# First weight block and tokens loaded, split and multiplied in four pieces; low parts of the next two blocks made by an adding DMA

## The reference

```python
def _rmsnorm(x, g):
    y = x * lax.rsqrt(jnp.mean(x * x, axis=-1, keepdims=True) + EPS)
    return y * g

def _swiglu(xn, w_in, w_out):
    gu = xn @ w_in                        # 1024 x 5632
    g, u = gu[..., :D_FF], gu[..., D_FF:]
    return (jax.nn.silu(g) * u) @ w_out

def _layer(x, ...):
    x = x + 0.5 * _swiglu(_rmsnorm(x, norm_ffn1), w_ffn1_in, w_ffn1_out)
    ...   # mLSTM, gated linear attention, conv + RG-LRU, merged through w_out
    x = x + 0.5 * _swiglu(_rmsnorm(x, norm_ffn2), w_ffn2_in, w_ffn2_out)
```

## Time and profile before

| | us |
|---|---|
| median of three runs | 3015.81 |
| profiled execution | 3016.17 |
| its span, first to last instruction | 3014.0 |
| PE busy | 2953.7 (98%) |
| DVE busy | 2272.4 (75%) |
| ACT busy | 1340.8 (44%) |
| POOL busy | 12.9 |

### The profile page before, as it was taken

One profiled execution on the slowest core, in us unless ns is written; L12 is line 12 of the kernel. 1 busy time (PEld: TensorE's weight loads), 2 busy tenths in 40 slices (PEclk: granted clock), 3 DMA queues, 4 the chain that ended last, 5 costly groups with the idle time before them and its releaser, 6 DMA issues.

```text
span 3014.0 us, 59955 instructions
## 1 busy us (share of the span) xinstructions
PE 2953.7 (98%) x24960; PEld 2904.6 (96%) x24960; DVE 2272.4 (75%) x3371; ACT 1340.8 (44%) x1733; POOL 12.9 (0%) x36
## 2 busy tenths in 40 slices
PE   8999999999999999999999999999999999999998
PEld 8999999999999999999999999999999999999997
DVE  8685777778788878585785857776878888695766
ACT  5463533334335655363553635333334466453543
POOL 1000000000000000000000000000000000000000
PEclk9999999999999999999999999999999999999999
DMA  3222332323222222232322323233222222222322
GB/s 131 104 98 91 98 109 97 131 96 112 99 89 94 80 83 85 94 103 84 104 78 98 106 97 98 95 127 122 94 93 96 94 91 91 86 78 91 112 84 72
DMA packets 60151, 292.73 MB, mean 97 GB/s; under 512 B 9385, under 2 KB 12265, under 8 KB 32073
## 3 DMA queue, kind: packets, MB, share of 16 engines
q1 hardware_dynamic: 45344, 241.43, 23.7%
q10 hardware_dynamic: 13984, 48.48, 4.4%
q0 software_dynamic: 656, 0.52, 0.1%
HBM read 268.90 MB, written 21.50 MB: 96 GB/s over the span
## 4 chain that ended last, share of the span: by engine, by line
PE 85%; DVE 9%; ACT 3%; issue 1%; DMA 1%; DVEq 0%; ACTq 0%; POOL 0%; POOLq 0%
PE stream_b L477 23%; PE stream_a L477 23%; PE mix L546 11%; PE stream_b L546 6%; PE stream_a L546 5%; PE stream_a L624 5%; PE mix L477 3%; DVE wl L1449 1%; PE mix L909 1%; PE stream_b L630 1%; PE mix L745 1%; PE mix L685 1%; DVE wl L1528 1%; PE mix L829 1%; PE mix L666 1%
## 5 line engine op out<-in xcount | busy, mean ns | idle before, releaser
L1449 DVE TENSOR_TENSOR wl<-stage,wh 128x2048 fp32r<-128x2048 f32 (+1 forms) x148 | 332.7, 2248 | 91.2 <-ACT wh L969 67.0
L969 ACT ACTIVATE wh<-stage 128x2048 fp32r<-128x2048 f32 (+1 forms) x134 | 252.1, 1882 | 318.6 <-PE stream_b L477 221.7
L477 PE MATMUL stream_a<-xh,wh 128*128 128x272 f32 x1280 | 271.0, 293 | 15.6 <-DVE xl L1455 13.2
L477 PE MATMUL stream_b<-xh,wh 128*128 128x272 f32 x1280 | 276.1, 297 | 0.0
L477 PE MATMUL stream_a<-xl,wh 128*128 128x272 f32 x1280 | 265.5, 289 | 0.0
L477 PE MATMUL stream_a<-xh,wl 128*128 128x272 f32 x1280 | 264.9, 288 | 0.0
L477 PE MATMUL stream_b<-xl,wh 128*128 128x272 f32 x1280 | 264.9, 288 | 0.0
L477 PE MATMUL stream_b<-xh,wl 128*128 128x272 f32 x1280 | 264.2, 288 | 0.0
L477 PEld LDWEIGHTS stream_a<-xh,wh 128*128 128x128 f32 x1280 | 202.6, 189 | 18.6 <-DVE wl L1449 13.1
L477 PEld LDWEIGHTS stream_b<-xh,wh 128*128 128x128 f32 x1280 | 201.8, 188 | 7.3 <-issue 3.3
L477 PEld LDWEIGHTS stream_a<-xh,wl 128*128 128x128 f32 x1280 | 201.9, 189 | 0.0
(11 more groups left out here) (435 smaller groups left out, 8598.1 us busy)
## 6 DMA issues: line engine op xcount, KB each, us to landing
stage<-in_w_mix SPq DMA_DIRECT2D x88, 1024.0 KB, 4.9
stage<-in_w_up SPq DMA_DIRECT2D x87, 1024.0 KB, 4.9
stage<-in_w_down SPq DMA_DIRECT2D x16, 1024.0 KB, 5.0
stage<-in_w_down SPq DMA_DIRECT2D x32, 512.0 KB, 4.5
stage<-in_w_down SPq DMA_DIRECT2D x16, 768.0 KB, 4.4
CS<-in_c ACTq DMA_DIRECT2D x8, 1024.0 KB, 4.8
out_o_sc<-CS ACTq DMA_DIRECT2D x8, 1024.0 KB
CS<-in_s ACTq DMA_DIRECT2D x8, 1024.0 KB, 4.9
```

The source lines that it names most:

```text
L477: mm = [pe.matmul(out(h), a(h), b(h), start=f, stop=z) for h in range(2)]
L969: act.activation(wh[:, slot, 0:width], stage[:, slot, 0:width], ACT.Copy).then_inc(hi_done, 1)
L1449: tt_(wl[:, slot, 0:width], stage[:, slot, 0:width], wh[:, slot, 0:width].bitcast(F32), ALU.subtract).then_inc(split_done, 1)
```

## The change

SP now issues the first loads, behind that of the vectors: block 0 in four pieces of two k steps and the tokens in four pieces of two k steps, by turns. ACT no longer issues them; its first instruction is a tiny copy, which brings the first load of its function table forward. ACT and DVE split piece by piece, first two k steps of weights, then two of tokens. TensorE takes block 0 k step by k step, both output tiles in each, when that k step's low token part is there (`first_low`), and sums the squares inside block 1 (`second_block`) and no longer inside block 0.

DVE splits block 1 before it adds the squares from the third on, and ACT makes the high part of block 1 after the third square.

For blocks 2 and 3 of this first network (`f == 0`), ACT writes the negated high part into `wl` and then the high part into `wh`. POOL waits for the first of these and issues a DMA that adds `stage` onto `wl` in SBUF, waits until it has landed, and counts `split_done`. DVE's two subtractions of 128 x 2048 are gone there.

```diff
+FIRST = 4
+FIRST_K = KT // FIRST
...
         def _(sp):
             sp.dma_start(V[:], vec).then_inc(vec_loaded, 16)
+            for p in range(FIRST):
+                piece = slice(p * FIRST_K * 2 * P, (p + 1) * FIRST_K * 2 * P)
+                sp.dma_start(stage[:, 0, piece], w_up1[0, 0][:, piece]).then_inc(
+                    first_loaded[p] if p < FIRST - 1 else block_loaded[0], 16)
+                part = slice(p * FIRST_K, (p + 1) * FIRST_K)
+                sp.dma_start(x[:, part, :], x_T[:, part, :]).then_inc(x_loaded[p], 16)
...
-                        sp.wait_ge(x_loaded[1], 16)
+                        sp.wait_ge(x_loaded[FIRST - 1], 16)
                         load(1, 1, w_up[L, 1])
...
             pool.dma_start(m0t[:], m0).then_inc(const_loaded, 16)
+            for k in range(2):
+                pool.wait_ge(minus_high, k + 1)
+                pool.dma_start(wl[:, k, :], stage[:, k, :], accum_op=ALU.add).then_inc(lows_landed, 16)
+                pool.wait_ge(lows_landed, k * 16 + 16)
+                pool.wait_ge(hi_done, k + 3)
+                pool.memset(token[:, k:k + 1], 0.0).then_inc(split_done, 1)
...
-            def first_block(n, t, j, norm):
+            def first_block(n, t, j):
+                for k in range(KT):
+                    pe.wait_ge(first_low, k + 1)
+                    for e in range(2):
+                        tile(t + e, e, KT, 2 * P, e * P, weights=(wh[:, j], wl[:, j]), ks=[k])
+
+            def second_block(n, t, j, norm, root):
                 parts = (wh[:, j], wl[:, j])
                 block_ready(n)
-                tile(t, 0, KT, 2 * P, 0, weights=parts, low=first_low)
-                tile(t + 1, 1, KT, 2 * P, P, weights=parts, ks=range(KT // 2))
+                tile(t, 0, KT, 2 * P, 0, weights=parts, out=four[2], free=2, ks=range(2))
                 pe.wait_ge(acc_ready, norm)
                 norm_squares().then_inc(norm_sum, 1)
-                tile(t + 1, 1, KT, 2 * P, P, weights=parts, ks=range(KT // 2, KT))
+                tile(t, 0, KT, 2 * P, 0, weights=parts, out=four[2], ks=range(2, KT))
+                pe.wait_ge(sd_ready, root + 1)
+                tile(t + 1, 1, KT, 2 * P, P, weights=parts, out=four[3], free=2)
...
             act.wait_ge(init_done, 1)
-            act.dma_start(stage[:, 0, :], w_up1[0, 0]).then_inc(block_loaded[0], 16)
-            for h in range(2):
-                part = slice(h * (KT // 2), (h + 1) * (KT // 2))
-                act.dma_start(x[:, part, :], x_T[:, part, :]).then_inc(x_loaded[h], 16)
+            act.activation(sdT[:], sdT[:], ACT.Copy)
...
-            def split_hi(nh, slot, through, width):
+            def split_hi(nh, slot, through, width, minus=False):
                 act.wait_ge(block_loaded[slot], nh * 16 + 16)
                 act.wait_ge(tile_done, through + 3)
+                if minus:
+                    act.activation(wl[:, slot, 0:width], stage[:, slot, 0:width], ACT.Copy,
+                                   scale=-1.0).then_inc(minus_high, 1)
                 act.activation(wh[:, slot, 0:width], stage[:, slot, 0:width], ACT.Copy).then_inc(hi_done, 1)
...
+            first_pieces()
+            first_squares(range(3))
+            act.wait_ge(block_loaded[1], 16)
+            act.activation(wh[:, 1, :], stage[:, 1, :], ACT.Copy).then_inc(hi_done, 1)
+            first_squares(range(3, KT))
...
-                                split_hi(nh + 1, i, t + 2 * i + 1, 2 * D)
+                                split_hi(nh + 1, i, t + 2 * i + 1, 2 * D, minus=f == 0)
...
-                        split_lo(n + 2, 0, 2 * D)
+                        if f:
+                            split_lo(n + 2, 0, 2 * D)
...
-                        split_lo(n + 3, 1, 2 * D)
+                        if f:
+                            split_lo(n + 3, 1, 2 * D)
```

More of the change, by code:

```diff
@@ L153, in trunk @@
         zero_t = sb("zero_t", [P, 1])
+        token = sb("token", [P, 2])
         acc = sb("acc", [P, N])
@@ L257, in trunk @@
         const_loaded = sem("const_loaded")
-        x_loaded = [sem("x_loaded_0"), sem("x_loaded_1")]
+        x_loaded = [sem(f"x_loaded_{p}") for p in range(FIRST)]
+        first_loaded = [sem(f"first_block_loaded_{p}") for p in range(FIRST - 1)]
+        first_high = sem("first_high_parts")
+        minus_high, lows_landed = sem("minus_high_parts"), sem("low_parts_landed")
         vec_loaded = sem("vec_loaded")
@@ L511, in norm_squares @@
                 return mm
-            def first_block(n, t, j, norm):
+            def first_block(n, t, j):
[4 more added lines that the diff above has]
+            def second_block(n, t, j, norm, root):
                 parts = (wh[:, j], wl[:, j])
                 block_ready(n)
-                tile(t, 0, KT, 2 * P, 0, weights=parts, low=first_low)
-                tile(t + 1, 1, KT, 2 * P, P, weights=parts, ks=range(KT // 2))
+                tile(t, 0, KT, 2 * P, 0, weights=parts, out=four[2], free=2, ks=range(2))
                 pe.wait_ge(acc_ready, norm)
                 norm_squares().then_inc(norm_sum, 1)
-                tile(t + 1, 1, KT, 2 * P, P, weights=parts, ks=range(KT // 2, KT))
+                tile(t, 0, KT, 2 * P, 0, weights=parts, out=four[2], ks=range(2, KT))
+                pe.wait_ge(sd_ready, root + 1)
+                tile(t + 1, 1, KT, 2 * P, P, weights=parts, out=four[3], free=2)
             def ffn_in_block(L, n, t, j, norm=None, rooted=None):
                 if norm == KT:
-                    return first_block(n, t, j, norm)
+                    return first_block(n, t, j)
+                if rooted == (1, 0):
+                    return second_block(n, t, j, KT, 0)
                 block_ready(n)
@@ L976, in _, with first_pieces @@
             act.wait_ge(vec_loaded, 16)
-            def first_high(slot):
-                act.wait_ge(block_loaded[slot], 16)
-                act.activation(wh[:, slot, :], stage[:, slot, :], ACT.Copy).then_inc(hi_done, 1)
+            def first_pieces():
+                for p in range(FIRST):
+                    piece = slice(p * FIRST_K * 2 * P, (p + 1) * FIRST_K * 2 * P)
+                    act.wait_ge(first_loaded[p] if p < FIRST - 1 else block_loaded[0], 16)
+                    act.activation(wh[:, 0, piece], stage[:, 0, piece], ACT.Copy).then_inc(
+                        first_high if p < FIRST - 1 else hi_done, 1)
+                    act.wait_ge(x_loaded[p], 16)
+                    for m in range(p * FIRST_K, (p + 1) * FIRST_K):
+                        high_part(m, V_FIRST + m)
             def first_squares(ms):
@@ L1727, in _ @@
             dve.wait_ge(vec_loaded, 16)
-            split_lo(0, 0, 2 * D)
-            for m in range(KT // 2):
-                low_part(m, V_FIRST + m, m, first_low)
+            for p in range(FIRST):
+                piece = slice(p * FIRST_K * 2 * P, (p + 1) * FIRST_K * 2 * P)
+                if p < FIRST - 1:
+                    dve.wait_ge(first_high, p + 1)
+                else:
+                    dve.wait_ge(hi_done, 1)
+                ins = tt_(wl[:, 0, piece], stage[:, 0, piece], wh[:, 0, piece].bitcast(F32), ALU.subtract)
+                if p == FIRST - 1:
+                    ins.then_inc(split_done, 1)
+                for m in range(p * FIRST_K, (p + 1) * FIRST_K):
+                    low_part(m, V_FIRST + m, m, first_low)
             dve.wait_ge(sq_ready, 2)
             link(tt_(acc[:], first_sq[0], first_sq[1], ALU.add))
-            for m in range(KT // 2, KT):
-                low_part(m, V_FIRST + m, m, first_low)
+            split_lo(1, 1, 2 * D)
             for m in range(2, KT):
@@ L1741, in _ @@
             dve.wait_ge(acc_ready, KT)
-            split_lo(1, 1, 2 * D)
             def decay_rates():
```

## The result

The changed kernel takes 3024.89 us (median, 3024.22 to 3026.9) against 3016.61 for the kernel before, measured beside it: a ratio of 1.0028, 95% interval 1.0019 to 1.0036, so 8.3 us slower. The forecast was 3.2 us slower and called that within 0.2%; the time lies at the upper end of the range, and the loss is clear of noise.

A forecast was written before the change was run, and what follows sets the result against it. TensorE, busy 98% of the span, was taken as the bound, through its start of block 2: +1.5 us (42.0, not 40.5) plus 1.7 for its clock, +3.2, giving 3019.0 us by the median; range 3013.0 to 3025.0.

The forecast's parts named there:

- the gap in block 1: PE, two k steps into block 1, was to stop from 23.0 to 25.4 us for the norm's sum.
- the lower clock behind the gaps: PE was to fall to 1.2 GHz after each gap over some 2 us, costing 1.7 us each.
- block 3's add hidden: Block 3's adding DMA was to start about 45 us and land at 53, before PE needed it at 54 or later.
- The loads: First loads from SP: same bytes issued 0.64 us sooner, so the last token piece was to land at 11.5 us.
- The norm's sum: PE's sum of squares in block 1 was put at about 25.4 us, with negation starting 7.07 us later at 32.5.
- The add: Block 2's adding DMA was put at 7.3 us plus 0.3 for POOL, making block 2 ready at 42.0.
- The clock at block 2: After standing some 4 us ahead of block 2, PE was to lose 1.7 us to its lower clock.
- the copy-like add: Rival at block 2: the adding DMA takes 4.9 us like a copy, 0.9 us shorter, 3014.9 us; chance 0.22.
- Slow adding: Rival at block 2: DMA adds slower than it copies, passing 0.2% slower at 10.1 us, up to 3024.7; chance 0.16.
- The pieces did come one by one: Judged rival on first loads: eight pieces land together at 11.5 us, block 2 ready at 45.5, 3022.5 us; chance 0.07.
- DVE's relief in full: Rival in the fast blocks: 4.57 us less DVE work shortens their beginning, 5.5 us gained, 3010.3 us; chance 0.07.
- The first part on what is removed: Dropping DVE's first 2.28 us split was to give nothing, since its next operation needs ACT's `hh`.

The follow-up runs named there:

- coarse loads: Changed kernel with SP loading block 0 whole and the tokens in two halves, the splits still in pieces: 3023.02 us, ratio 1.0022 to the kernel before.
- block whole: The kernel of "one add early" with block 0 loaded whole and the tokens still in four pieces: 3012.50 us, ratio 0.9983 to the kernel before.
- the run with the copy: Changed kernel with a plain copy of the block in place of the adding DMA, leaving out the subtraction: 3020.28 us (one run).
- squares first: Changed kernel with the squares and their additions ahead of block 1's split on ACT and DVE, the adding DMA kept: 3022.34 us, ratio 1.0018.
- weights in pieces with token halves: Changed kernel with block 0 still loaded in four pieces but the tokens in two halves: 3025.88 us (one run).
- add alone: Kernel before with only the adding DMA for blocks 2 and 3 put in, loads and first blocks as they were: 3017.61 us, ratio 1.0004.
- one add early: The kernel of "norm in block 0" plus the adding DMA for block 3 alone, both ACT passes over it moved ahead of a SiLU: 3012.41 us, ratio 0.9987.
- no add: Changed kernel with the adding DMA undone, DVE splitting blocks 2 and 3 again: 3021.44 us, ratio 1.0014 to the kernel before.
- no add, squares first: Changed kernel with the adding DMA undone and the squares ahead of block 1's split: 3017.77 us, ratio 1.0002 to the kernel before.
- norm in block 0: The kernel of "no add, squares first" with PE summing the squares at the end of block 0, not inside block 1: 3014.78 us, ratio 0.9994.

## Why the prediction was right or wrong

Right was the reading of what decides: PE's start of block 2, the way there through norm, negation and add, the gap in block 1, the lower clock behind the gaps, block 3's add hidden, and the shift reaching the end. Three experiments bear the mechanism out: without the squares' delay, with a cheaper transfer and with earlier loads, block 2 moved by 3.24, 2.93 and 1.93 us, and the medians by 2.6, 4.6 (one run, with the clock's price gone too) and 1.9.

Wrong was the size, 3.2 against 8.05 us at the end of block 3, in four terms of the sum that all erred the same way; the loads are the largest:

- *The loads.* "The bytes are the same, so the last token piece lands at 12.15 - 0.64 = 11.5": it landed near 13.7 (SP's next issue). This is the step that failed first and by most: it took the time of the loads from their bytes alone and put cutting them into pieces at nothing. The norm's sum followed, 27.47 against 25.4: +2.1 us. The runs with coarse loads and with the block whole, which issue block 1 at 11.77 and 11.66, show that 11.5 was right for these bytes with block 0 in one transfer, and that the weight pieces were not priced. PE's first matmul, forecast near 7 us, came at 9.30, since the first tokens were there at 7.68 and not at 5.5; that cost nothing, as PE's start is not on the chain.
- *The norm's sum.* I let the gap ahead of it cool the clock, but charged that to block 1, where PE has time, and not to the sum, which stands on the chain. From its start to the negation it was 8.12 us, not 7.07: +1.05. (The 24.29 from which the 7.07 were read is the loading of its weights; the sum itself starts at 24.57, so 6.79 us was the way at the upper clock. Of the 1.33 us more, 1.27 are the sum's own 2.19 in place of 0.92.)
- *The add.* 8.68 us from the end of the negation to PE's start, in place of 7.6: +1.1. The copy shows the fixed part and one passage to be 4.60, near the 4.9 taken; the adding was undersized, 3.6 us where one passage of 2.45 was put.
- *The clock at block 2.* 2.4 us in place of 1.7: +0.7. The price at the kernel's start was the nearer row.

2.1 + 1.05 + 1.1 + 0.7 is 4.95, against 4.85 between forecast and measurement at 72.66.

The rivals: the copy-like add is excluded by the run with the copy, 4.60 us where the add takes 8.19. Slow adding came true in part: 8.2 us, short of the 10.1 that alone would have cost 0.2%. The pieces did come one by one, so that rival's mechanism was wrong, but its effect, a late norm, made about half of the loss: the reciprocal stands 4.23 us later. DVE's relief in full did not happen in this kernel, yet I argued it away too far: "that stretch begins at PE's end of block 3" holds only while PE is late there. With the add undone, DVE set the time in three kernels, and its relief by one split was worth 2.4 us in the last step (3014.78 to 3012.41; 1.6 by the fixed group).

The first part on what is removed stands as predicted: DVE waited 1.96 us for ACT's `hh` at 39.87, so the first dropped split gave next to nothing (this operation starts 9.19 us behind the reciprocal; before it was 9.34):

```profile
39.87 0.72 DVE L1525 TENSOR_TENSOR hl<-gs,hh 128x544 fp32r<-128x544 f32 x1 [1.96 <-ACT hh L1054]
```

## What to carry to other kernels

An earlier start is worth only what the next thing on the chain moves: here PE began 3.9 us sooner and stood 8.2 us afterwards, because what it needed next had become later: the last tokens by the pieces, the norm's sum by the split put ahead of it, and block 2 by the add. Take work off a busy engine with a slower, parallel path only where the result is needed late (block 3, 12 us of cover, gain 2.4 us), not where it is the next thing awaited (block 2). When a wait of some microseconds is added to TensorE, whose clock fell behind such waits here, charge the slow matmuls to whatever stands directly behind the wait, and ask whether that is on the chain.

## What the runs showed of the hardware

- An adding DMA from SBUF to SBUF moved 1 MB (block 2, changed kernel) at 262 GB/s at most, a copy of the same shape at 413 over its 2.5 busiest microseconds; from issue to landing 8.19 against 4.60 us. The first add landed in 8.18 to 8.19 us in four kernels (changed, squares first, coarse loads, weights in pieces with token halves), in 7.04 in two (add alone, one add early) and in about 7.4 in one (block whole). PE was at work until near the landing in the faster three and stood idle in the four. That alone does not decide it: the second add of the changed kernel, with PE at work throughout, took about 8.5 us, though the load of block 4 ran beside it. The cause stays open.
- A quarter of block 0 as the first transfer arrived little earlier than the whole block: ACT's first copy began at 5.74 to 6.21 with the quarter and at 6.30 to 6.55 with the whole, after the table load in all. The quarters read rows of 2 KB, the whole rows of 8 KB, and between 3 and 4.5 us the engines moved about 100 GB/s with the quarters. By 5 us 0.47 MB had moved in the changed kernel (a sum of half-microsecond stretches), so that more than half of block 0 was still to come, and from 5.5 to 12 us the engines moved 355 to 441 GB/s with these quarters among the rest. This speaks against the row length by itself; what makes the first small transfers slow stays open.
- PE's granted clock fell to 0.5 behind single waits of 2.54 us (changed kernel), 2.64 and 2.72 (no add), 2.78 (no add, squares first) and 5.61 to 6.02. It stayed at 1.00 behind waits of 0.28 us (add alone), 0.53 (copy), 0.93 (no add, squares first) and 1.62 (norm in block 0). Four matmuls of the norm's sum took 2.19 us at the lower level, where 0.92 and 0.93 are the times at the upper.
